# Moving the scaling of attention probabilities to ScalarE and re-timing the modulation tiles in a two-layer encoder

## What is computed

```python
mod = c_act @ ada_w[l] + ada_b[l]                 # 6 x 1024 modulation values, ada_w[l] is 1024 x 6144
sh1, sc1, g1, sh2, sc2, g2 = jnp.split(mod[:, None, :], 6, axis=-1)
h = _rmsnorm(x, norm_mix_g[l]) * (1.0 + sc1) + sh1
z = h @ even_w_in[e]                              # 1024 x 4096
o_a = _hgrn2(z[..., :5 * A_WIDTH], ...)           # gated linear recurrence, both directions
o_b = _neighbourhood_attention(q_b, k_b, v_b, rpb)  # 8 heads, softmax over a window of the grid
mixed = jnp.concatenate([o_a, o_b], axis=-1) @ even_w_out[e]
x = x + g1 * mixed
x = x + g2 * _conv_ffn(_rmsnorm(x, norm_ffn_g[l]) * (1.0 + sc2) + sh2, ...)
```

## Time and profile before

| | |
|---|---|
| median of 3 runs | 800.9 us (799.97 to 802.1) |
| the profiled execution | 799.51 us, span 797.8 us |
| mean granted TensorE clock | 0.962 |
| TensorE busy | 746.7 us (94%) |
| VectorE busy | 578.6 us (73%) |
| ScalarE busy | 421.5 us (53%) |
| GpSimd busy | 77.6 us (10%) |

### The profile page before, as it was taken

How to read it: one execution, slowest core, us unless ns; L and a number is a source line. 1 busy time by engine, 2 the same in 40 slices (tenths; PEclk the granted TensorE clock), 3 DMA queues, 4 the chain that set the end, 5 groups by cost and what they waited for, 6 DMA issues and landing times.

```text
span 797.8 us, 16703 instructions
## 1 busy us (share of the span) xinstructions
PE 746.7 (94%) x6637; PEld 722.9 (91%) x6637; DVE 578.6 (73%) x792; ACT 421.5 (53%) x664; POOL 77.6 (10%) x95
## 2 busy tenths in 40 slices
PE   3799999589989999999989999998898999999997
PEld 3798899579989999999979998897798999999997
DVE  4858987696689999766656779966467788886342
ACT  4453669212466666663344564556446676666332
POOL 2201000005000110001010006200004000000001
PEclk9599999889989999999998999999998999999999
DMA  8999656843539999667575987763144888755501
GB/s 329 372 322 314 218 162 213 283 145 106 144 103 289 291 286 289 230 224 284 185 256 164 329 281 245 244 217 107 53 131 114 237 257 247 234 203 209 190 22 53
DMA packets 161393, 171.24 MB, mean 215 GB/s; under 512 B 5453, under 2 KB 142358, under 8 KB 161344
## 3 DMA queue, kind: packets, MB, share of 16 engines
q1 hardware_dynamic: 154112, 145.23, 57.3%
q0 software_dynamic: 7232, 25.33, 8.9%
HBM read 169.49 MB, written 1.05 MB: 214 GB/s over the span
## 4 chain that ended last, share of the span: by engine, by line
PE 74%; DVE 11%; DMA 7%; ACT 3%; issue 3%; SPq 2%; DVEq 0%; ACTq 0%
PE acc L1328 52%; PE big L1328 13%; DVE w_lo L880 4%; DMA ada_raw<-in_ada_w 4%; DMA w_raw<-in_even_w_in 2%; DVE mod_acc L890 2%; ACT w_hi L572 2%; SPq L349 2%; DVE qk L336 1%; DMA w_raw<-in_even_w_out 1%; PE aux L1437 1%; DVE mod_acc L1198 1%; PE big L1437 1%; PE big L1522 1%; DVE stat L1281 1%
## 5 line engine op out<-in xcount | busy, mean ns | idle before, releaser
L1328 PE MATMUL acc<-h_hi,w_hi 128*128 128x256 f32 x1248 | 353.2, 283 | 10.6 <-DVE h_lo L932 6.1
L1328 PE MATMUL acc<-h_lo,w_hi 128*128 128x256 f32 x1248 | 349.5, 280 | 0.0
L1328 PE MATMUL acc<-h_hi,w_lo 128*128 128x256 f32 x1248 | 349.1, 280 | 0.0
L880 DVE TENSOR_TENSOR w_lo<-w_raw,w_hi 128x1024 fp32r<-128x1024 f32 x218 | 266.2, 1246 | 87.5 <-ACT w_hi L572 87.5
L572 ACT ACTIVATE w_hi<-w_raw 128x1024 fp32r<-128x1024 f32 x220 | 224.5, 1050 | 101.2 <-PE acc L1328 84.1
L1328 PEld LDWEIGHTS acc<-h_hi,w_hi 128*128 128x128 f32 x1248 | 238.9, 191 | 14.2 <-issue 9.7
L1328 PEld LDWEIGHTS acc<-h_lo,w_hi 128*128 128x128 f32 x1248 | 239.2, 192 | 0.0
L1328 PEld LDWEIGHTS acc<-h_hi,w_lo 128*128 128x128 f32 x1248 | 238.8, 191 | 0.0
L1328 PE MATMUL big<-hid_hi,w_hi 128*128 (+1 forms) x308 | 85.6, 278 | 0.0
L1328 PE MATMUL big<-hid_lo,w_hi 128*128 (+1 forms) x308 | 85.2, 277 | 0.0
L1328 PE MATMUL big<-hid_hi,w_lo 128*128 (+1 forms) x308 | 85.2, 276 | 0.0
(11 more groups left out here) (245 smaller groups left out, 898.7 us busy)
## 6 DMA issues: line engine op xcount, KB each, us to landing
w_raw<-in_ffn_w_up SPq DMA_DIRECT2D x88, 512.0 KB, 5.0
ada_raw<-in_ada_w POOLq DMA_DIRECT2D x48, 512.0 KB, 5.5
w_raw<-in_ffn_w_down SPq DMA_DIRECT2D x44, 512.0 KB, 4.0
w_raw<-in_odd_w_in SPq DMA_DIRECT2D x40, 512.0 KB, 5.3
w_raw<-in_even_w_in SPq DMA_DIRECT2D x32, 512.0 KB, 8.1
ada_raw<-in_ada_w SPq DMA_DIRECT2D x28, 512.0 KB, 4.0
ada_first<-in_ada_w SPq DMA_DIRECT2D x12, 512.0 KB, 13.0
w_raw<-in_even_w_out SPq DMA_DIRECT2D x8, 512.0 KB, 8.4
```

Of the source, the lines that this page charges most:

```text
L880: dve.tensor_tensor(w_lo[:, n % SPLIT, part], w_raw[:, n % RAW, part], w_hi[:, n % SPLIT, part].bitcast(F32), ALU.subtract).then_inc(s_lo, ...
L1328: ins = pe.matmul(dst, lhsT, rhs, start=start and n == 0, stop=stop and n == 2, skip_group_check=True)
```

## The change

ScalarE takes over the multiplication of the probabilities (`attend_scale`), right behind the exponential or the copies of the step, and VectorE keeps only the reciprocal, with a new semaphore `weight_ready`. VectorE adds two tiles at each p from 5 to 10, and one at 11 to 14, none at 15. GpSimd issues 20 tiles and SyncE 4, each behind one of the loads of EO to EO+3. VectorE's products of the gates (`qk`, L1079) move from p = 14 to p = 13, and `own_k` and they go ahead of the tiles of their p.

```diff
-ADA1_POOL = 16
-EVEN_TILES = (1, 2, 1, 2, 2, 1, 1, 1, 1, 2, 2, 2, 2, 2, 1, 1)
+ADA1_POOL = 20
+EVEN_TILES = (1, 2, 1, 2, 2, 2, 2, 2, 2, 2, 2, 1, 1, 1, 1, 0)
...
+        weight_ready = sem("weight_ready")
...
-            for tile in range(ADA1_POOL, ADA2 - ADA1):
-                rest_tile(tile)
             for n in range(N_EO):
                 load(0, EO + n, columns(even_w_out[0])[:, :, n * 256:(n + 1) * 256])
+                rest_tile(ADA1_POOL + n)
...
+            def attend_scale(r):
+
+                if 0 <= r < PAIRS:
+                    act.wait_ge(weight_ready, r + 1)
+                    if r >= 2:
+                        act.wait_ge(turned, 2 * r - 2)
+                    for b in (0, 1):
+                        nc.scalar.activation(ns[:, 2 * (r % 2) + b, :], big[:, 2 + r % 2, b * T:(b + 1) * T], ACT.Copy,
+                                             scale=pstat[:, r % 4, 2, b:b + 1]).then_inc(out_taken, 1)
...
                     attend_copies(s)
                     if s % 2 == 0:
                         attend_exp(s)
+                    attend_scale(s - 1)
...
                     dve.wait_ge(exp_done, 2 * r + 2)
-                    link(dve.reciprocal(pstat[:, r % 4, 2, :], pstat[:, r % 4, 1, :]))
-                    if r >= 2:
-                        dve.wait_ge(turned, 2 * r - 2)
-                    for b in (0, 1):
-                        dve.tensor_scalar(ns[:, 2 * (r % 2) + b, :], big[:, 2 + r % 2, b * T:(b + 1) * T], pstat[:, r % 4, 2, b:b + 1], None,
-                                          ALU.mult).then_inc(out_taken, 1)
+                    dve.reciprocal(pstat[:, r % 4, 2, :], pstat[:, r % 4, 1, :]).then_inc(weight_ready, 1)
...
-                for _ in range(left):
-                    add_first(next(tiles))
                 if p == 12:
                     dve.wait_ge(gate_act, GATES_SPLIT)
                     dve.tensor_tensor(own_k, qk[:, 0, :], qk[:, 3, :], ALU.add)
-                if p == 14:
+                if p == 13:
                     dve.wait_ge(gate_act, Q_SCALED)
                     for d in (0, 1):
                         ins = dve.tensor_tensor(qk[:, 1 + d, :], qT, fT[1 - d], ALU.mult)
                     ins.then_inc(own_ready, 1)
+                for _ in range(left):
+                    add_first(next(tiles))
+                if p == 14:
                     split_lo(0, EO)
```

## The result

| | before | changed |
|---|---|---|
| median of 20 runs | 804.75 us (798.84 to 812.48) | 797.63 us (794.49 to 802.49) |
| ratio | 1 | 0.9935, 95% interval 0.991 to 0.996 |
| profiled execution | 799.51 us | 801.91 us; once more: 796.12 us |

The change makes the kernel faster by 0.65%, or 5.2 us of 804.75, with an interval of 3.2 to 7.2 us. I forecast 6.4, and 794.5 us as the time. The two medians lie 7.1 us apart; I go by the ratio and its interval.

A forecast was written before the change was run, and what follows sets the result against it. TensorE sets the pace, losing most in an 8.0 us wait before the recurrence. With the stall, 0.5 us back and tile 23's chain, `grow` of level 1 moves from 163.97 to 157.5: 6.4 us, 800.9 to 794.5, range 791.8 to 799.0.

The forecast's parts named there:

- What bounds, and the queue: End of layer 0's projection: TensorE's 8.0 us wait goes except 0.65 us; a chain through tile 23 then decides.
- The tile's landing: End of the projection: tile 23 leaves SP at 144.1 and takes 5.5 us to land; bounds 3.8 and 7.
- The stall in unit 7: Attention units: ScalarE's first scaling delays taking unit 6; TensorE stands still 1.75 us once, bounds 0 and 8.7 us.
- the slacks I feared for: Unit 8: scaling 3 ends 0.2 us before TensorE's transposes, scaling 4 ends 0.3 us before the unit's taking.
- The end of the projection: At p = 11 to 13 VectorE has fewer tiles, so `split_lo` no longer makes TensorE wait: 0.5 us back.
- The clock: Start of the recurrence: with a pause of 0.7 us instead of 8.0, TensorE's clock should stay 1.00; no gain added.
- The sum: `grow` of level 1 starts at 157.5 against 163.97: gain 6.4 us, median from 800.9 to 794.5.
- (1): Tile 23 is not late, landing in 3.8 us: gain 8 to 9 us, 792.3 us; chance 0.18.
- (2): ScalarE's order bites in every attention unit: losing 0.8 us in each of five leaves 2.4 gain, 798.5; chance 0.15.
- (3): Tiles land late in the attention units, needing over 7.6 us; at 8.0 us slower, 806.5 us; chance 0.07.

The follow-up runs named there:

- the runs at full clock: First pair scaled by VectorE, on the changed kernel with tile 23 ahead of EO+3's load; ratios 0.9919 and 0.9856, recurrence 24.29 and 24.30 us.

## Why the prediction was right or wrong

What failed is the size of two terms, not the path: tile 23's landing, priced at 5.5 us, took 6.7, and the low clock in the recurrence, priced at nothing, cost 0.8 to 1.3 us.

**What bounds, and the queue: right.** The 8.0 us of TensorE are 0.7 now, and a new chain through tile 23 decides, as put: split of unit 15, three DMAs, landing, add, split of EO, total. Moving one line of the queue took 4.8 us out of it.

**The tile's landing: the term that was mis-sized.** I had it leave at 144.1 and take 5.5 us; it left at 144.65 and took 6.7 (the two tiles before it, each behind a load of EO too, 5.8). With the start of the first units taken out that is 0.3 and 1.2 us, which makes the total start at 154.66 on the clock of before, against 153.15 foretold. Part of it is my own adding up: 3.7 and 3 less 0.9 are 5.8, not 5.5. The other 0.9 us stay open; the loads issued behind the tile are ruled out. The bounds, 3.8 to 7, held it.

**The stall in unit 7: right.** 1.75 us foretold, 1.5 us of waits and 1.7 of delay measured. Two scalings take 0.84 us, 1.7 us a unit for the 1.6 from L621's row, and the slacks I feared for (0.2 and 0.3 us) were enough. The Trainium skill, "ScalarE: Activation LUTs", "Step-by-step: what each stage is for", calls PSUM the faster port; no run here writes this result to PSUM, so what SBUF costs isn't shown. Giving the scaling back to VectorE made each unit 0.6 us longer where I had said 0.5.

**The end of the projection: right.** `split_lo` no longer makes TensorE wait, and unit 14 is taken 0.9 us later than before (144.33 with 0.23 for the start) instead of 1.7: 0.8 back, foretold 0.5.

**The clock: wrong.** I wrote that it should stay at 1.00 behind a pause of 0.7 us. Behind that pause it did, and the first 64 products took 2.08 us. But my own sum had TensorE 3 us ahead of VectorE right behind it, and I drew nothing from that. TensorE waited 4.0 us there and was granted 0.50 from 157 to 161 and 0.66 after. My sum shortened the recurrence by 0.6 us, from 24.89 to 24.3, which is what the runs at full clock need; the changed kernel needed 25.55, and 25.08 in its first profile.

**The sum.** Foretold 6.4; in the trace the total is 4.4 us earlier (4.14 and 0.23 for the start) where 5.9 was foretold, 1.5 less because of the tile. The recurrence took 1.25 more than foretold, and 3.7 are left: the span ends 3.4 us earlier, 3.6 with the start. The measured ratios say 5.2 (3.2 to 7.2) and 4.7 us. The mechanism was right and the size too large. That the stated 794.5 us lies only 1 us from the 795.4 of the quickest group owes something to luck, since by the two profiles less than 4 us was gained; the twenty runs leave open which of the two sizes is nearer.

**The rivals.** None took the place of the forecast. Tile 23 was late (1), ScalarE's order bit once (2), and no tile was late in the attention units (3): from 85 to 120 us VectorE waits for none. Not a rival either, though it should have been, was the low clock behind TensorE's wait for VectorE. What else I missed was that parts of the change are worth nothing alone: the queue alone, or all but the tile counts, give 1.001 and 1.002.

## What to carry to other kernels

When a queue is reordered, ask of each transfer that is now behind another what waits for it last, and try the neighbouring order: one line, tile 23 ahead of EO+3, took 5.8 us off the span of the profile, where the whole change had taken 3.4 (by the ratios, whose intervals are as wide as that, about as much again). Moving work to the engine with idle time pays only through what takes the freed time; and the first time round, before the pipeline is full, the moved step stands ahead of work that others wait for. A pause that moves takes its low clock along, and it costs where another engine then waits for TensorE.

## What the runs showed of the hardware

A unit of 48 products of 256 columns takes either 5.44 or 5.65 us, at a granted clock of 1.00 both times, for a whole stage, and not every stage of an execution shares it: in the first profile of the changed kernel layer 0's next stage ran at 5.65 and layer 1's at 5.44, and in the second profile both at 5.44. In the profile of the queue alone both ran at 5.65, though its projection ran at 5.44, and that execution is the longest of its kernel. Timeline of ScalarE's first instruction of two units in the next stage of layer 0, in the first profile and then in the second:

```profile
227.57 0.56 ACT L767 ACTIVATE conv<-acc,vecs 128x256 f32<-128x256 f32 x1 [2.66 <-PE acc L1335]
233.22 0.56 ACT L767 ACTIVATE conv<-acc,vecs 128x256 f32<-128x256 f32 x1 [1.78 <-PE acc L1335]
```

```profile
227.83 0.56 ACT L767 ACTIVATE conv<-acc,vecs 128x256 f32<-128x256 f32 x1 [3.23 <-PE acc L1335]
233.27 0.56 ACT L767 ACTIVATE conv<-acc,vecs 128x256 f32<-128x256 f32 x1 [1.57 <-PE acc L1335]
```

0.21 us times 22 units is 4.6 us, most of the 6 us by which the runs of one kernel differ. The granted clock doesn't show it, and what sets it is open. So a time from three runs is not known better than that, and traces are compared stage by stage, after a look at the pace.
